# Row norms of a two-block network on one core: sums by token in four columns, spread by one product, and the first two tiles by turns

## The reference

```python
def rms_norm(x, gain):
    y = x * lax.rsqrt(jnp.mean(x * x, axis=-1, keepdims=True) + EPS)
    return y * gain
# first block (h: 16 meta tokens + 512 tokens)
hn = rms_norm(h, attn_norm);   h = h + fox_mixer(hn, ...)        # 16 heads of 64
h = h + swiglu(rms_norm(h, ffn_norm), w_in, w_out)               # hidden width 2816
h = rms_norm(h, final_norm)[:, N_META:]
# second block
n1 = _rmsnorm(h, norm1_g) * (1.0 + sc1) + sh1
#   mixer: causal convolution of 31 taps -> _layernorm -> silu -> @ w_cv_out
#          SSM branch y -> _rmsnorm over 4 groups of 512 -> @ w_ssm_out
#          (gated sum of both) @ w_mix_out
h = h + g1 * mixer(n1)
n2 = _rmsnorm(h, norm2_g) * (1.0 + sc2) + sh2
h = h + g2 * hier_moe(n2)          # 64 experts, 2 for a token; x @ w1, x @ w3, @ w2
return _rmsnorm(h, final_g)
```

## Time and profile before

| | |
|---|---|
| median of three runs | 2738.35 us (2738.22 to 2742.57) |
| the profiled execution | 2741.23 us, its span 2739.3 us |
| PE busy | 2392.8 us (87%) |
| PE weight loads | 1444.7 us (53%) |
| DVE busy | 861.4 us (31%) |
| ACT busy | 756.9 us (28%) |
| POOL busy | 784.4 us (29%) |
| mean granted TensorE clock | 0.94 |
| a 1 MB load of ffn weights, issue to landing | 7.7 us, median of 22 |

### The profile page before, as it was taken

The page is one execution under the profiler, slowest core; times in us unless marked ns, Lnnn a source line. Parts: engine busy times, 40 slices in busy tenths (PEclk is TensorE's granted clock), DMA queues, the critical chain, the costliest instruction groups (busy, mean ns, idle before and its releaser), DMA issues.

```text
span 2739.3 us, 26286 instructions
## 1 busy us (share of the span) xinstructions
PE 2392.8 (87%) x10854; PEld 1444.7 (53%) x10854; DVE 861.4 (31%) x1329; ACT 756.9 (28%) x1194; POOL 784.4 (29%) x500
## 2 busy tenths in 40 slices
PE   6999899899998899579989699798888888888895
PEld 4676556678886578457767486332223222332231
DVE  2533451200002599724667512311101110111103
ACT  3333452322222233244666522200000000000001
POOL 3232543444553344133332353310100101010100
PEclk8999999899999799789999899899999999999998
DMA  3344212342223233213333434799999999999995
GB/s 138 123 148 149 80 42 93 123 154 91 94 70 112 81 93 77 74 42 127 108 123 108 168 143 160 259 421 426 426 425 427 426 425 425 425 424 423 425 422 221
DMA packets 165047, 597.27 MB, mean 218 GB/s; under 512 B 15875, under 2 KB 81411, under 8 KB 139328
## 3 DMA queue, kind: packets, MB, share of 16 engines
q1 hardware_dynamic: 148320, 562.23, 52.6%
q10 hardware_dynamic: 5936, 23.89, 2.2%
q0 software_dynamic: 10672, 9.46, 1.1%
HBM read 591.00 MB, written 28.96 MB: 226 GB/s over the span
## 4 chain that ended last, share of the span: by engine, by line
PE 52%; DMA 27%; DVE 13%; ACT 4%; issue 1%; POOL 1%; SPq 0%; ACTq 0%; DVEq 0%; POOLq 0%
DMA arena<-in_w 22%; PE ps L706 11%; PE ps L707 11%; PE ps L708 11%; PE ps L1132 7%; DVE ps L1924 4%; DMA ring<-in_w 3%; PE ps L725 2%; DVE scr L1695 1%; PE ps L1130 1%; PE ps L1151 1%; ACT arena L1234 1%; PE ps L743 1%; PE ps L842 1%; DMA ring<-in_w_in 1%
## 5 line engine op out<-in xcount | busy, mean ns | idle before, releaser
L2308 POOL TENSOR_TENSOR ring_r<-ring,ring_r 128x1024 fp32r<-128x1024 f32 (+2 forms) x220 | 514.3, 2342 | 761.8 <-ACT ring_r L1223 761.5
L706 PE MATMUL ps<-r,ring_r 128*128 128x512 f32 (+1 forms) x1632 | 655.6, 402 | 59.3 <-POOL r L2319 48.1
L707 PE MATMUL ps<-r,ring_r 128*128 128x512 f32 (+1 forms) x1632 | 645.7, 396 | 0.0
L708 PE MATMUL ps<-r,ring_r 128*128 128x512 f32 (+1 forms) x1632 | 645.4, 395 | 0.0
L1234 ACT ACTIVATE arena<-ps 128x512 f32<-128x512 f32 (+4 forms) x279 | 188.0, 693 | 1234.2 <-PE ps L1132 868.7
L1132 PE MATMUL ps<-arena 128*64 128x512 f32 x672 | 325.5, 642 | 75.0 <-DMA arena<-in_w 74.7
L706 PEld LDWEIGHTS ps<-r,ring_r 128*128 128x128 f32 (+1 forms) x1632 | 310.8, 190 | 147.1 <-issue 63.9
L708 PEld LDWEIGHTS ps<-r,ring_r 128*128 128x128 f32 (+1 forms) x1632 | 310.8, 190 | 68.9
L707 PEld LDWEIGHTS ps<-r,ring_r 128*128 128x128 f32 (+1 forms) x1632 | 311.3, 191 | 66.5 <-issue 1.9
L1130 PE MATMUL ps<-arena 128*64 128x512 f32 x672 | 332.2, 643 | 0.0
L1223 ACT ACTIVATE ring_r<-ring 128x1024 fp32r<-128x1024 f32 (+2 forms) x220 | 222.9, 1015 | 360.8 <-PE ps L708 261.6
(11 more groups left out here) (303 smaller groups left out, 2168.0 us busy)
## 6 DMA issues: line engine op xcount, KB each, us to landing
arena<-in_w SPq DMA_DIRECT2D x105, 2048.0 KB, 36.2
ring<-in_w SPq DMA_DIRECT2D x87, 2048.0 KB, 37.6
ring<-in_w_ada SPq DMA_DIRECT2D x12, 2048.0 KB, 13.3
ring<-in_ffn_w_in SPq DMA_DIRECT2D x22, 1024.0 KB, 7.7
ring<-in_w_in SPq DMA_DIRECT2D x40, 512.0 KB, 6.0
ring<-in_fox_w_in SPq DMA_DIRECT2D x8, 2048.0 KB, 8.5
ring<-in_w_in SPq DMA_DIRECT2D x8, 2048.0 KB, 9.7
ring<-in_ffn_w_out SPq DMA_DIRECT2D x4, 2048.0 KB, 7.9
```

The lines of the kernel that those rows point to most:

```text
L706: e.matmul(out, wh[:, k, :], X.hi[:, k0 + k, :], start=first and k == 0, stop=False)
L707: e.matmul(out, wh[:, k, :], X.lo[:, k0 + k, :], start=False, stop=False)
L708: m = e.matmul(out, wl[:, k, :], X.hi[:, k0 + k, :], start=False, stop=last and k == nk - 1)
L2308: e.tensor_tensor(GL[t], grans[t][1], GH[t].bitcast(F32), ALU.subtract).then_inc(sem["gr_lo"], 1)
```

## The change

- **Sums by token.** A row of sums is now four products: each takes 128 tokens of the squares as the stationary side and one column of ones as the moving side (789), so the sums of 512 tokens stand as 128 partitions by 4 columns. A product with zeros closes the group (797). ACT's root and DVE's reciprocal then work on 128x4 (1833). A one-element Sqrt ahead of the wait loads the table early (not for gn 0 to 2).
- **Spread.** DVE multiplies the identity by the four columns into a 128x512 tile (`diagonal`, 1827), and one product with the matrix of ones (`spread`, 808) puts the factors into PSUM, from where DVE's multiplications read them.
- **Sums between tiles.** The rows of fn go behind `op` tiles 2 to 7, 12 of the 16 of `fin` between the last `fo` tiles, those of n2 behind `mo` tiles 2 to 7.
- **Final norm and norm 1 in one.** The squares are summed with and without the final gain in one pass; the root of a combination gives norm 1's factor. `x2` is written without its factor while the `fo` tiles come; the factor of the final norm (`rx`) is spread later, and the residual is multiplied by it in the `so` loop (eight DVE operations more).
- **First two tiles by turns.** `pair` takes the first two tiles of each normed input k by k: six products for each k. The meta tile `km` 0 of the first stage moves behind the pair.
- **Rests.** The subtraction of the rests is divided anew: x k=0,1,3,5,7 and fn and ln odd k on DVE, n1 all on DVE, in a form that adds the shift and subtracts in one (ACT adds the shift in its rounding copy).
- **Fillers.** In attention 2, 0, 0, 1 products for m mod 4 instead of 2 each; two in front of a spread and four or five behind it elsewhere (761).
- The root of ln goes ahead of `early_gate(4)` on ACT.

```diff
+            def pair(uses, X, k0=0, first=True, last=True):
+                gs = [granule() for _ in uses]
+                nk = gs[0][1].shape[1]
+                if first:
+                    for use in uses:
+                        w.wait_ge(use.free, use.n)
+                for k in range(nk):
+                    w.wait_ge(*X.ready(k0 + k))
+                    for use, (_, wh, wl) in zip(uses, gs):
+                        e.matmul(use.ap, wh[:, k, :], X.hi[:, k0 + k, :], start=first and k == 0, stop=False)
+                        e.matmul(use.ap, wh[:, k, :], X.lo[:, k0 + k, :], start=False, stop=False)
+                        m = e.matmul(use.ap, wl[:, k, :], X.hi[:, k0 + k, :], start=False, stop=last and k == nk - 1)
+                        if k == nk - 1:
+                            m.then_inc(use.full if last else sem["gr_used"], 1)
...
-            def sum_row(name, k, nk, segs, src, uses, mat):
-                rows0, sums0 = sums[name]
-                w.wait_ge(sem["sq"], rows0 + k + 1)
-                for u, (s0, n) in zip(uses, segs):
-                    if k == 0:
-                        w.wait_ge(u.free, u.n)
-                    m = e.matmul(u.ap[:, :n], mat, src[:, s0:s0 + n], start=k == 0, stop=k == nk - 1)
-                    if k == nk - 1:
-                        m.then_inc(u.full, 1)
-                if k < nk - 1:
-                    m.then_inc(sem["sq_used"], 1)
-            def sum_rows(name, nk, segs, *keys):
-                for k in range(nk):
-                    sum_row(name, k, nk, segs, TMP[k % 2], [ps(*key) for key in keys], ones)
+            def sum_row(name, j, nk, off=0):
+                rows0, _ = sums[name]
+                u = ps(*name) if type(name) is tuple else ps(name)
+                w.wait_ge(sem["sq"], rows0 + j + 1)
+                if j == 0:
+                    w.wait_ge(u.free, u.n)
+                    if name == "x":
+                        w.wait_ge(ps("xq").free, ps("xq").n)
+                for tt in range(4):
+                    rows = TMP[j % 2][:, off + 128 * tt:off + 128 * tt + 128]
+                    out, by = u.ap[:, tt:tt + 1], ones[:, 0:1]
+                    if name == "fin":
+                        both = u.ap[:, 0:8].rearrange("p (s t) -> p t s", s=2)[:, tt, :]
+                        out, by = (both, C("one_eps")) if j % 2 == 0 else (u.ap[:, 4 + tt:5 + tt], by)
+                    m = e.matmul(out, rows, by, start=j == 0 and tt == 0, stop=False)
+                if name == "x":
+                    m = e.matmul(ps("xq").ap[0:NM, 0:1], TMP[j % 2][:, 0:NM], ones[:, 0:1], start=j == 0, stop=j == nk - 1)
+                    if j == nk - 1:
+                        m.then_inc(ps("xq").full, 1)
+                if j == nk - 1:
+                    n = 8 if name == "fin" else 4
+                    m = e.matmul(u.ap[:, 0:n], ones[0:1, :], C("zero", 0, 1)[:, 0:n], start=False, stop=True)
+                m.then_inc(u.full if j == nk - 1 else sem["sq_used"], 1)
+            def sum_rows(name, nk, off=0):
+                for j in range(nk):
+                    sum_row(name, j, nk, off)
+            def spread(name, *key):
+                u = ps(*key)
+                w.wait_ge(sem["dg"], diags[name])
+                w.wait_ge(u.free, u.n)
+                e.matmul(u.ap, ones, RST[:, :T], start=True, stop=True).then_inc(u.full, 1)
...
+            spread("x", "xb")
...
+            fill(5, "k", 0)
+            pair([ps("k", 0), ps("k", 1)], XN)
...
-                    filler(PS[64:128, 7, 0:256], 2)
+                    filler(PS[64:128, 7, 0:256], (2, 0, 0, 1)[m % 4])
...
-            sum_rows("fn", 8, SEGT, ("fn",))
+                if nt >= 2:
+                    sum_row("fn", nt - 2, 8)
+            sum_row("fn", 6, 8)
+            sum_row("fn", 7, 8)
+            fill(2, "fnb")
+            spread("fn", "fnb")
+            fill(4, "hg", 0)
+            pair([ps("hg", 0), ps("hu", 0)], XF)
...
+                            i = 8 * c + r // 2 + j
+                            rows = {9: 0, 10: 1, 11: 2, 12: 3, 14: 4, 15: 5}
+                            if half == 1 and i in rows:
+                                sum_row("fin", 2 * rows[i], 16)
+                                sum_row("fin", 2 * rows[i] + 1, 16)
+            for j in range(12, 16):
+                sum_row("fin", j, 16)
+            fill(2, "finb")
+            spread("fin", "finb")
+            fill(4, *conv_tiles(0)[0])
...
+            pair([ps(*key) for key in conv_tiles(0)[0:2]], X1)
...
+            sum_rows("ln", 8)
+            fill(2, "lnb")
+            spread("ln", "lnb")
             whole("eg", 4, X=X1)
             whole("eg", 5, X=X1)
-            for nt in range(8):
+            pair([ps("co", 0), ps("co", 1)], XC)
+            for nt in range(2, 8):
                 whole("co", nt, X=XC)
...
+            fill(2, "gnb", 3)
+            spread(("gn", 3), "gnb", 3)
+            spread("rx", "rx")
+            fill(4, "so", 0)
+            pair([ps("so", 0), ps("so", 1)], XY[1], last=False)
...
-            def root(uses, segs, scale):
-                for u, (s0, n) in zip(uses, segs):
-                    evict(RST[:, s0:s0 + n], u, ACT.Sqrt, src=u.ap[:, :n], scale=scale, bias=C("eps"))
+                e.activation(TMP[k % 2][:, :n], src, ACT.Square, scale=gain).then_inc(sem["sq"], 1)
+            def root(u, name, nk, early=True):
+                if name != "x":
+                    w.wait_ge(sem["dg"], diags[name] - 1)
+                if early:
+                    e.activation(ST[:, 12:13], C("eps"), ACT.Sqrt)
+                return evict(ST[:, 0:4], u, ACT.Sqrt, src=u.ap[:, 0:4], scale=1.0 / nk, bias=C("eps"))
...
+            def squares_fin(k):
+                square_after(ps("fo", 1, k), "fin", 2 * k, hT[:, k, NM:L])
+                square_row("fin", 2 * k + 1, hT[:, k, NM:L], T, pc("final_norm", k))
...
+            e.activation(ST[:, 12:13], C("eps"), ACT.Sqrt)
+            u = ps("fin")
+            w.wait_ge(sem["dg"], diags["fin"] - 1)
+            w.wait_ge(u.full, u.n + 1)
+            e.activation(ST[:, 4:8], u.ap[:, 4:8], ACT.Sqrt, scale=1.0 / D, bias=C("eps2"))
+            evict(ST[:, 8:12], u, ACT.Sqrt, src=u.ap[:, 0:4], scale=1.0 / D, bias=C("eps"))
             w.wait_ge(sem["x2"], 8)
             e.dma_start(a["x2_d"], x2).then_inc(sem["spill"], 16)
             for k in range(8):
-                square_row("n1", k, x2[:, k, :], T)
-            root([ps("n1")], SEGT, 1.0 / D)
-            for k in range(8):
                 w.wait_ge(sem["n1"], k + 1)
-                e.activation(n1H[:, k, :], TMP[k % 2][:, :T], ACT.Copy).then_inc(sem["n1_hi"], 1)
+                e.activation(n1H[:, k, :], TMP[k % 2][:, :T], ACT.Identity, bias=modcol(0, k)).then_inc(sem["n1_hi"], 1)
...
+            root(ps("ln"), "ln", D)
             early_gate(4)
             early_gate(5)
...
-            root([ps("ln")], SEGT, 1.0 / D)
...
+            def diagonal(r):
+                return e.tensor_tensor(cols(RST[:, :T], 4), cols(ident, 1).broadcast_to([128, 4, 128]),
+                                       r.rearrange("p (a b) -> p a b", b=1).broadcast_to([128, 4, 128]), ALU.mult).then_inc(sem["dg"], 1)
+            def factors(u, ub, r):
+                w.wait_ge(u.free, u.n + 1)
+                e.reciprocal(r, r).then_inc(d.next(), 1)
+                last()
+                diagonal(r[:, 0:4])
+                w.wait_ge(ub.full, ub.n + 1)
+                return ub.ap
...
...
-            root_inverse([ps("n1")], T)
             w.wait_ge(sem["x2"], 8)
+            ub = ps("finb")
+            r = factors(ps("fin"), ub, ST[:, 4:12])
+            def low_n1(k):
+                w.wait_ge(sem["n1_hi"], k + 1)
+                e.scalar_tensor_tensor(n1L[:, k, :], TMP[k % 2][:, :T], modcol(0, k), n1H[:, k, :].bitcast(F32), ALU.add, ALU.subtract).then_inc(lows["n1", k][0], 1)
             for k in range(8):
-                x = TMP[k % 2][:, :T]
                 if k >= 2:
-                    w.wait_ge(sem["n1_lo"], k - 1)
-                e.scalar_tensor_tensor(x, x2[:, k, :], SC[:, k:k + 1], RST[:, :T], ALU.mult, ALU.mult).then_inc(d.next(), 1)
-                last()
-                e.tensor_scalar(x, x, modcol(0, k), None, ALU.add).then_inc(sem["n1"], 1)
+                    w.wait_ge(*lows["n1", k - 2])
+                e.scalar_tensor_tensor(TMP[k % 2][:, :T], x2[:, k, :], SC[:, k:k + 1], r, ALU.mult, ALU.mult).then_inc(sem["n1"], 1)
+                if k >= 1:
+                    low_n1(k - 1)
+            w.wait_ge(sem["n1"], 8)
+            e.sem_inc(ub.free, 1)
+            low_n1(7)
...
+                e.tensor_tensor(x2b[:, nt, :], x2b[:, nt, :], ps("rx").ap, ALU.mult).then_inc(sem["x2r"], 1)
```

300 lines of the change are left out of this document (185 added, 115 removed).

## The result

| | before | changed |
|---|---|---|
| median, first comparison (four runs each) | 2740.41 us (2738.22 to 2742.57) | 2717.29 us (2708.46 to 2718.35) |
| ratio | | 0.9909, 95% interval 0.9885 to 0.9932 |
| the profiled execution, its span | 2741.23, 2739.3 | 2708.46, 2706.6 |

The changed kernel is 0.9% faster, 23 us of the 82 forecast. The forecast direction held, the size did not, and the time lies outside the range of 2630 to 2690. The profiled execution is the fastest of the four, 9 us under their median; where about half of that difference can lie is shown with the first experiment.

A forecast was written before the change was run, and what follows sets the result against it. It took TensorE's work (busy 87%) plus PE's waits as the bound, DVE in the convolution and DMA at the end. Terms summed to 82.3 us off 2741.2, so 2659; it said 2657, range 2630 to 2690.

The forecast's parts named there:

- x: First normed input: earlier factor and pair bring the third k tile from 58.0 to 44.5 us; 12.5 less taken (10 to 15).
- Attention: Five of eight filler products go, part of their time becoming waits for ACT; 12.4 us less (0 to 20).
- fn: Norm behind ada(8): five rows moved earlier, pair 11.5 us earlier, later weight loads limit it; 8.7 less (6 to 11.5).
- fin, n1: Final norm and norm 1 ahead of the convolution: 12 of 16 rows earlier, norms merged; 29.5 us less (24 to 33).
- ln: Norm ahead of the co tiles: root under the gate tiles, pair ends at 1209.5; 9.2 us less (5 to 11).
- gn: gn 0 to 2: DVE saves 3 us each, mostly off the path, PE pays 0.65 each; 3 less (2 more to 6 less).
- gn 3, so: Last gn and the so tiles: start moves by 3 us, the pair a little more; 3.5 less.
- n2: Between the last mo tile and the router: rows moved earlier shorten the 13.3 us gap; 3.5 less (2.4 to 5).
- Rival 1: Clock doesn't hold at the pairs of x, fn, n1, ln: about 6 us each, 24 together, 2681; chance 0.17.
- Rivals 2 and 4: Attention. 2: bound by ACT and DVE, 12.4 back, 2669, chance 0.10. 4: without fillers PE drops to 1.2 GHz, chance 0.04.
- Rival 3: Subtractions on DVE and POOL collide in x, fn, ln: 4 each by 1.0 us, 12 together, 2669; chance 0.10.
- Rival 5: Merged norm or order fails, or DVE's in-order queue delays gn and ln: gain 40 only, 2700; chance 0.06.

The follow-up runs named there:

- e1: The first experiment: the changed kernel with gn 0 to 2 alone back to wide rows of sums, without zero product or spread; median 2711.32 us, 0.9862 of before.
- e7: The changed kernel with 32 products of width 1 and 8 of 512 columns added between co tiles; 2721.68 us (one run).
- e12: The changed kernel with 128 equal columns of ones instead of one in all rows but fin's, zero product over 512 columns; median 2698.93 us, 0.9854 of before.
- e5: The changed kernel with gn 0 to 2 and ln back to wide rows, ln's early root and pair kept; median 2694.12 us, 0.9837 of before.
- e13: e5 with 128 columns in the rows of x, fn, gn 3 and n2, and fn without its pair; median 2685.83 us, 0.9799 of before.
- e10: The changed kernel with 32 products of 128 columns, 16 of 256, and 64 of width 1 with 128x32 weights added between co tiles; 2736.43 us (one run).

## Why the prediction failed

**The failed step is the price of the new operations on PE.** A row was taken at 0.9, "between 0.5 (half the records, if weights load under other work) and 1.05", the spread at "(one old row, 0.9)". Between tiles a row took 0.92 to 1.03 us, as forecast. In a row of rows it took 1.43 (fn), 1.22 (fin), 1.73 (ln), 0.93 to 1.75 (gn), 1.86 (x) and 0.93 (n2), and the spread mostly 2.08. The bounds from the earlier trace rows were taken at full clock and put on places where the new products themselves take the clock away; e7 shows that they do it, e12 that 128 columns in their place don't. With this go operations that the sum had at nothing: the zero product (0.58 us) stands in no term, and the term of ln has neither the spread nor the wait for ACT and DVE ahead of it, though both stand in front of the gate tiles.

How much is which: by the medians 60 us are missing (2717.3 against 2657). Giving the rows their pace back returned 18 of them (e12); taking rows, zero product and spread away at gn 0 to 2 and ln returned 23 (e5), the best of both 31 (e13). The rest is spread over the stages below and is argued from their rows, not shown by an experiment.

- **x**: 3.7 short. Rows and spread; with 128 columns the third tile is 12.4 earlier than before, which is the 12.5 of the sum.
- **Attention**: 2.1 short, the waits as forecast (1.01 and 0.50 us). Mechanism right. The forecast's own two waits, 0.55 and 0.48, add up to 1.03 and not to 0.97, which makes its term 11.9.
- **fn**: 5.4 short. Three rows at 1.43, the spread at 1.75, and a late load. The forecast gave 2.8 us to those of the third and fourth tile, but these tiles follow the pair at 5.4 us each, without a wait; the late one is that of ada(9), behind them: 3.4 us, and in some executions up to 5 more by the clock behind it.
- **fin, n1**: 4.1 short. Rows by 1.22, the zero product and the spread; the merging was priced right.
- **ln**: 11.4 off, 10.0 of it between tile 136 and 137: 4.6 the rows, 4.4 from their end to the end of the spread, 1.0 the slow first products of the gate tile. The pair gained 7.8, near the forecast.
- **gn**: 14.0 off in this trace. The forecast gave DVE's saving a price though PE was the bound there, and had 0.65 us for what PE does more in each group. At gn 0 the rows cost the forecast 0.93 each, and yet the stretch is 4.4 us longer: zero product 0.58, spread 2.08, and the products between and behind them at half pace (the 22 records ahead of the spread take 3.6 us, before 1.9). e1 shows that what was lost there is PE's own.
- **gn 3, so**: 2.6 short, **n2**: 6.8 off; the rows between mo tiles cost 4.6, and behind the last tile only 1.3 came back. Both lie near the scatter of these stretches.

Rival 1 had half clock in the right kernel and the wrong place: the pairs run at or near full pace (8 k of x in 11.2 us; granted 1.00 at fn from 470.5 to 484, 0.79 and then 1.00 at n1 from 870.5 to 885, 0.88 at ln from 1160 to 1172), the sums don't. Rivals 2 and 4 are refuted by attention's window (0.97, 1.01 us of wait). Rival 3 is not seen where it was placed: DVE's subtractions take 0.68 to 0.78 us in x and fn and 0.69 in ln, but for the last one, 1.37. In the so stage they take 1.76 to 1.79 beside POOL's, and did so before the change. Rival 5 named 2700, the nearest to the result, but its reason is not what is seen: at n1 and ln DVE starts on the root 0.1 us behind ACT, and gains there came; the loss lies on PE. ACT's table load shows no drain: in the kernel before, one ends at 1194.73 and the root's record starts at 1194.75, so the 1.38 us that the Trainium skill, page "ScalarE: Activation LUTs", section "What ACT_TABLE_LOAD costs", adds are not there.

Of the prediction's signs, the waits of the pair's first products for POOL or DVE are 9.7 us in sum, under the 15 named. The first product of the convolution pair stands at 873.4 and the first tap at 897.7, where 889.5 and 915 were named; but those two times leave out what the stages before had gained. Less the 22.0 us gained by then they would be 867.5 and 893, so both came 5 to 6 us late.

The Trainium skill, page "TensorE: Matmul & The Clock Gate", section "Terms", has a block that watches how busy PE is and gates its clock. The trace agrees that the clock follows the work, but its record of busy time doesn't show which level comes: it is full for ln's narrow rows (13.88 of 14 us, granted 0.50) and full for e5's wide ones (3.00 of 3.00, granted 0.84 and then 1.00).

## What to carry over

Price a product that moves few columns at both clock levels, and charge the work behind it too: the same row cost 0.95 us among full tiles and 1.73 in a run of its own kind. Where a float32 product loads 128x128 weights anyway, widening its moving side to 128 equal columns cost about 0.1 us a row at full clock and was worth 18 us here in all. List every new operation on the bounding engine, with the waits that it brings, also those too small to notice one by one. And before saving an engine's time, read whether the stage is bound by it: DVE's 3 us at gn paid nothing, PE's 4 us in exchange were paid in full.

## What the runs showed of the hardware

- Half pace does not always show in the granted clock: in x the column reads 1.00 while rows take 1.86 us, twice what they take at full pace.
- With 128x128 weights, a float32 product of 1 column takes 0.23 to 0.24 us at full clock (a row of four in 0.92 to 0.95) and 0.43 at half (ln's rows, granted 0.50). With 64 columns it takes 0.43 at half as well; with 128 it takes 0.23 (e10's insertion, granted 1.00) to 0.26 (between full tiles in e12).
- 32 such products of 1 column, put between full tiles, took the granted clock from 1.00 to 0.50 with no idle time before them (e7); 32 of 128 columns left it at 1.00 (e10).
- After a wait of 3.1 to 3.7 us at the same place, ahead of ada(9), PE stayed at full clock in four traces and came back at half in six, with the same code from the pair to there.
